# First gate weights next to x, Fox's decay columns as fp32r halves, small transfers on the weight queue, a Silu at the head of each expert slot

## The reference

```python
# first network, layer by layer
x = x + 0.5 * swiglu(rmsnorm(x, norm_g[l, 0]), ffn_w_in[l, 0], ffn_w_out[l, 0])   # width 2816
x = x + (hgrn2_mixer if l == 0 else fox_mixer)(rmsnorm(x, norm_g[l, 1]), ...)
x = x + 0.5 * swiglu(rmsnorm(x, norm_g[l, 2]), ffn_w_in[l, 1], ffn_w_out[l, 1])
# fox_mixer: q, k, v, g, z_f = split(h @ w_in)      # z_f: 16 columns, one per head
#   c = cumsum(log_sigmoid(z_f + b_f)); softmax(q.k * scale + c_t - c_s) @ v, times sigmoid(g)
# second network, layer by layer: nsa_mixer, then mla_mixer
x = layer_norm(ALPHA * x + concat(mixer(x), memory_attention(x)) @ w_out, ...)
x = layer_norm(ALPHA * x + hier_moe(x), ...)        # 4 groups of 4 experts, width 512
```

## Time and profile before

| | us |
|---|---|
| median of three runs | 2218.84 (2216.57 to 2220.15) |
| profiled execution, its own time | 2213.9 |
| its span, first to last instruction | 2212.0 |
| TensorE busy | 2097.1 (95%) |
| VectorE busy | 1481.5 (67%) |
| ScalarE busy | 1158.2 (52%) |
| mean granted TensorE clock | 0.984 of full speed |

### The profile page before, as it was taken

How to read it: one execution, slowest core, us unless ns; L and a number is a source line. 1 busy time by engine, 2 the same in 40 slices (tenths; PEclk the granted TensorE clock), 3 DMA queues, 4 the chain that set the end, 5 groups by cost and what they waited for, 6 DMA issues and landing times. The chain is left out here.

```text
span 2212.0 us, 36828 instructions
## 1 busy us (share of the span) xinstructions
PE 2097.1 (95%) x14195; PEld 1880.7 (85%) x14195; DVE 1481.5 (67%) x2246; ACT 1158.2 (52%) x1657; POOL 26.1 (1%) x34
## 2 busy tenths in 40 slices
PE   6999999999999999889999989999999989999997
PEld 6999898999999978779998977787778758778876
DVE  5655675665666644476564447789888466888896
ACT  4343533534444335474433336677776455777774
POOL 1000000000000020000000000000000000000000
PEclk9999999999999999999999979999999999999999
DMA  8555222654444533335455421599996515799991
GB/s 280 189 194 186 96 77 96 218 181 171 171 171 171 184 102 122 129 132 171 171 179 153 146 77 65 189 327 331 344 316 213 218 39 172 247 328 325 317 358 57
DMA packets 312310, 421.09 MB, mean 190 GB/s; under 512 B 7844, under 2 KB 266304, under 8 KB 312096
## 3 DMA queue, kind: packets, MB, share of 16 engines
q1 hardware_dynamic: 308864, 415.93, 55.2%
q10 hardware_dynamic: 2816, 2.38, 0.5%
q0 software_dynamic: 544, 1.62, 0.3%
HBM read 416.70 MB, written 1.05 MB: 189 GB/s over the span
## 5 line engine op out<-in xcount | busy, mean ns | idle before, releaser
L2869 DVE TENSOR_TENSOR w_lo<-weight_ring,w_hi 128x1024 fp32r<-128x1024 f32 x384 | 449.3, 1220 | 36.1 <-ACT w_hi L2718 31.2
L572 PE MATMUL banks<-x_hi,w_hi 128*128 128x256 f32 x1408 | 400.6, 285 | 9.2 <-DVE w_lo L525 8.0
L573 PE MATMUL banks<-x_lo,w_hi 128*128 128x256 f32 x1408 | 399.0, 283 | 0.0
L574 PE MATMUL banks<-x_hi,w_lo 128*128 128x256 f32 x1408 | 398.9, 283 | 0.0
L2718 ACT ACTIVATE w_hi<-weight_ring 128x1024 fp32r<-128x1024 f32 x384 | 382.2, 1053 | 21.4 <-PE banks L2605 21.4
L518 ACT ACTIVATE w_hi<-weight_ring 128x1024 fp32r<-128x1024 f32 x88 | 93.0, 1057 | 418.2 <-PE banks L574 418.0
L890 DVE TENSOR_TENSOR pieces<-weight_ring,pieces 128x512 fp32r<-128x512 f32 (+2 forms) x245 | 166.8, 689 | 177.4 <-ACT pieces L879 175.8
L572 PEld LDWEIGHTS banks<-x_hi,w_hi 128*128 128x128 f32 x1408 | 270.8, 192 | 11.6 <-DVE w_lo L525 8.9
L879 ACT ACTIVATE pieces<-weight_ring 128x512 fp32r<-128x512 f32 (+2 forms) x245 | 151.4, 627 | 228.6 <-PE banks L826 218.3
L573 PEld LDWEIGHTS banks<-x_lo,w_hi 128*128 128x128 f32 x1408 | 270.9, 192 | 0.1
L574 PEld LDWEIGHTS banks<-x_hi,w_lo 128*128 128x128 f32 x1408 | 270.8, 192 | 0.0
(11 more groups left out here) (367 smaller groups left out, 3890.6 us busy)
## 6 DMA issues: line engine op xcount, KB each, us to landing
weight_ring<-in_ffn_w_in SPq DMA_DIRECT2D x88, 1024.0 KB, 7.5
weight_ring<-in_moe_w_gate SPq DMA_DIRECT2D x64, 1024.0 KB, 6.5
weight_ring<-in_moe_w_up SPq DMA_DIRECT2D x64, 1024.0 KB, 9.0
weight_ring<-in_moe_w_down SPq DMA_DIRECT2D x64, 1024.0 KB, 11.0
weight_ring<-in_ffn_w_out SPq DMA_DIRECT2D x44, 1024.0 KB, 9.6
weight_ring<-in_hg_w_in SPq DMA_DIRECT2D x12, 1024.0 KB, 8.1
weight_ring<-in_fox_w_in SPq DMA_DIRECT2D x12, 1024.0 KB, 8.5
weight_ring<-in_nsa_w_in SPq DMA_DIRECT2D x10, 1024.0 KB, 8.0
```

What stands on the lines that cost most here:

```text
L572: pe.matmul(out, w_hi, m_hi, start=start, stop=False, skip_group_check=True)
L573: pe.matmul(out, w_hi, m_lo, start=False, stop=False, skip_group_check=True)
L574: return pe.matmul(out, w_lo, m_hi, start=False, stop=stop, skip_group_check=True)
L2869: dve.tensor_tensor(self.piece(s, p, self.w_lo), self.piece(s, p), self.piece(s, p, self.w_hi.bitcast(F32)), ALU.subtract).then_inc(sem[ki ...
```

## The change

- **Opening.** TensorE turns x0 before it waits for the rows, and the rows go to another buffer (`cat`). SyncE issues the three transfers of the first fill right behind x and waits for the rows after them; the gate half has a semaphore of its own. ScalarE starts with a Sqrt of zero, waits for the parameters after its first square, splits the gate half of the first tile between chunks 1 and 2 of the input, and the up half and the down weights after the last chunk. VectorE follows in the same order. TensorE's gate half waits for `gate_lo` alone.
- **Hgrn2.** The wait for the whole split input becomes a wait by chunk in the first tile.
- **Fox.** The decay columns are split once, ahead of the norm, and z is made with `pe_three`, two tiles per chunk of the input. Abs and Exp move from q2 to q1; Ln stays at q2. The root for q stands ahead of the Sigmoid of g0, no longer behind it. The eight bias transfers go from ScalarE at g3 to SyncE between the v fills and the output weights.
- **Nsa.** The eight pair transfers go to SyncE between the fill of w1 and that of q0; the eight key transfers go to SyncE ahead of the output weights.
- **Moe.** `act_slot` begins with a Silu of one column into an otherwise unused tile.

The diff, without blank lines, most unchanged lines, and declarations of semaphores:

```diff
@@ -246,6 +246,7 @@
...
+    self.table = f32("table", [P, 1])
@@ -289,7 +290,10 @@
...
+    self.wz_split = f32("fox_w_z_split", [P, 2, KD, FOX_H], F32R)
...
+    self.first_gate, self.gate_hi, self.gate_lo = s("first_gate"), s("gate_hi"), s("gate_lo")
+    self.root_of_zero = f32("root_of_zero", [P, 1])
@@ -336,9 +340,9 @@
...
-    self.rows = k.sq[:].rearrange("p k t -> p (k t)")[:, 0:P]
-    self.pe_rows = k.sq[:].rearrange("p k t -> p (k t)")[0:32, P:2 * P]
-    k.banks.plan("params", "x0", "x1", "x2", "x3")
+    self.rows = k.cat.rearrange("p k t -> p (k t)")[:, 0:P]
+    self.pe_rows = k.cat.rearrange("p k t -> p (k t)")[0:32, P:2 * P]
+    k.banks.plan("x0", "params", "x1", "x2", "x3")
@@ -347,8 +351,6 @@
...
-    eng.wait_ge(k.rows_ready, 12 * 16)
 def act_dma(self, eng):
@@ -384,13 +386,12 @@
     for q in range(4):
-        out = b.claim(pe, f"x{q}") if q else None
-        if q == 0:
+        if q == 1:
             pe.wait_ge(k.rows_ready, 12 * 16)
...
             b.filled(pe.transpose(out[:, P:P + 32], self.pe_rows, k.ident[0:32, 0:32]), "params")
-            out = b.claim(pe, "x0")
+        out = b.claim(pe, f"x{q}")
         for n in range(4):
@@ -398,16 +399,19 @@
 def dve(self, dve):
     k, b = self.k, self.k.banks
-    src = b.wait(dve, "params")
-    dve.tensor_copy(k.param[:, 0:N_ROWS], src[:, 0:N_ROWS])
-    b.read(dve.tensor_copy(k.pe_cols[:], src[:, P:P + 32]), "params")
     for q in range(4):
...
         ins.then_inc(k.x_ready, 1)
+        if q == 0:
+            dve.wait_ge(k.x_ready, 1)
+            b.release(dve, "x0")
+            src = b.wait(dve, "params")
+            dve.tensor_copy(k.param[:, 0:N_ROWS], src[:, 0:N_ROWS]).then_inc(k.params_ready, 1)
+            b.read(dve.tensor_copy(k.pe_cols[:], src[:, P:P + 32]), "params")
     dve.wait_ge(k.x_ready, 4)
-    for q in range(4):
+    for q in range(1, 4):
         b.release(dve, f"x{q}")
@@ -499,12 +503,66 @@
-    with eng.Fori(0, turns) as i:
+    if not self.j0:
+        self.first_load(eng)
+        for f in range(1, half):
+            load(f, 0, 0)
+    with eng.Fori(0 if self.j0 else 1, turns) as i:
         for f in range(half):
...
+def first_load(self, eng):
+    k, r, n = self.k, self.k.ring, self.fills[0]
+    r.wait_free(eng, n)
+    slot, full = r.slot(n), r.full[n % SLOTS]
+    wg, wu, wd = self.sources(0, 0)
+    eng.dma_start(slot[:, 0:2048].rearrange("p (k n) -> p k n", k=KD), wg).then_inc(k.first_gate, 16)
+    eng.dma_start(slot[:, 2048:4096].rearrange("p (k n) -> p k n", k=KD), wu).then_inc(full, 16)
+    eng.dma_start(slot[:, 4096:6144].rearrange("p (j n) -> p j n", j=2), wd).then_inc(full, 16)
+    eng.wait_ge(k.rows_ready, 12 * 16)
+def first_tile(self, w, part):
+    half = slice(part * KD * P, (part + 1) * KD * P)
+    if w is None:
+        raw = self.k.ring.slot(self.fills[0])[:, part * 2048:(part + 1) * 2048]
+        return raw.rearrange("p (k n) -> p k n", n=256)[:, :, 0:P]
+    return w[:, 0, half].rearrange("p (k n) -> p k n", n=P)
+def act_first_gate(self, act):
+    k = self.k
+    act.wait_ge(k.first_gate, 16)
+    act.sem_inc(k.ring.full[self.fills[0] % SLOTS], 16)
+    act.wait_ge(k.gu_ready, 1)
+    act.activation(self.first_tile(k.w_hi, 0), self.first_tile(None, 0), ACT.Copy).then_inc(k.gate_hi, 1)
+def act_first_rest(self, act):
+    k = self.k
+    k.ring.wait_full(act, self.fills[0])
+    act.activation(self.first_tile(k.w_hi, 1), self.first_tile(None, 1), ACT.Copy).then_inc(k.gu_hi, 1)
+    act.wait_ge(k.out_used, 1)
+    raw = k.ring.slot(self.fills[0])[:, 4096:4096 + D]
+    act.activation(k.w_hi[:, 0, 2048:3072], raw, ACT.Copy).then_inc(k.out_hi, 1)
+def dve_first_gate(self, dve):
+    k = self.k
+    dve.wait_ge(k.gate_hi, 1)
+    dve.tensor_tensor(self.first_tile(k.w_lo, 0), self.first_tile(None, 0), self.first_tile(k.w_hi.bitcast(F32), 0),
+                      ALU.subtract).then_inc(k.gate_lo, 1)
+def dve_first_rest(self, dve):
+    k = self.k
+    dve.wait_ge(k.gu_hi, 1)
+    dve.tensor_tensor(self.first_tile(k.w_lo, 1), self.first_tile(None, 1), self.first_tile(k.w_hi.bitcast(F32), 1),
+                      ALU.subtract).then_inc(k.gu_lo, 1)
+    self.dve_split_out(dve, 0, 0)
@@ -575,9 +633,12 @@
 def pe_gate_up(self, pe, b, base, first=False):
     k = self.k
-    pe.wait_ge(k.gu_lo, base + 1)
+    if self.j0 or not first:
+        pe.wait_ge(k.gu_lo, base + 1)
     pe.wait_ge(k.h_ready, base + 1)
     for part in range(2):
+        if first and not self.j0:
+            pe.wait_ge(k.gu_lo if part else k.gate_lo, 1)
         for kk in range(KD):
@@ -626,14 +687,20 @@
         tiles = slice(2 * c, 2 * c + 2)
+        if not self.j0 and c == 2:
+            self.act_first_gate(act)
         act.wait_ge(k.x_ready, 4 * (self.turn - 1) + c + 1)
         act.activation(k.sq[:, tiles], k.x[:, tiles], ACT.Square).then_inc(k.norm_sq, 1)
+        if not self.j0 and c == 0:
+            act.wait_ge(k.params_ready, 1)
         for kk in (2 * c, 2 * c + 1):
...
 def dve_input(self, dve):
...
     for c in range(4):
+        if not self.j0 and c == 2:
+            self.dve_first_gate(dve)
         for kk in (2 * c, 2 * c + 1):
@@ -648,9 +715,12 @@
 def act(self, act):
...
         self.act_split(act, 0, self.j0, 0)
+    else:
+        act.wait_ge(self.k.zero_ready, 1)
+        act.activation(self.k.root_of_zero[:], self.k.zeros[:, 0:1], ACT.Sqrt)
     self.act_input(act)
     if not self.j0:
-        self.act_split(act, 0, self.j0, 0)
+        self.act_first_rest(act)
     self.act_std(act)
@@ -676,8 +746,7 @@
     if not self.j0:
-        self.dve_split_gu(dve, 0, self.j0)
-        self.dve_split_out(dve, 0, self.j0)
+        self.dve_first_rest(dve)
     dve.wait_ge(k.norm_std, self.ffn + 1)
@@ -1101,10 +1170,9 @@
 def pe(self, pe):
...
     self.norm.pe(pe)
-    self.pe_wait_input(pe)
     for part in "zq":
         for n in range(4):
-            self.pe_columns(pe, f"hg_{part}{n}")
+            self.pe_columns(pe, f"hg_{part}{n}", self.in_split if part == "z" and n == 0 else None)
     i = 0
@@ -1541,18 +1609,25 @@
                       ).then_inc(k.ring.full[n % SLOTS], 16)
+    eng.wait_ge(self.c_ready, 5)
+    eng.wait_ge(self.bias_ready, 4)
+    for half in range(2):
+        for row, to, src in ((0, self.bq, self.c_hi), (1, self.bq, self.c_lo), (32, self.bk, self.n_hi), (33, self.bk, self.n_lo)):
+            row += half * HD
+            eng.dma_start(to[row:row + 1].bitcast(F32), src[half:FOX_H:2, :].bitcast(F32)).then_inc(self.bias_rows, 16)
     self.sp_out(eng)
 def pe(self, pe):
...
     self.norm.pe(pe)
-    self.pe_wait_input(pe)
-    pe.wait_ge(k.small_ready, k.small_all)
+    pe.wait_ge(self.wz_ready, 2)
     out = b.claim(pe, "fox_z")[0:FOX_H, 0:T]
     for kk in range(KD):
-        for part in range(2):
-            last = pe.matmul(out, k.wz[:, kk], k.half[1 - part][:, kk].bitcast(F32), start=kk == 0 and part == 0,
-                             stop=kk == KD - 1 and part == 1)
+        if kk % 2 == 0:
+            pe.wait_ge(k.xs_lo, 4 * self.in_split + kk // 2 + 1)
+        last = self.pe_three(pe, out, (k.wz_split[:, 0, kk], k.wz_split[:, 1, kk]), (k.half[1][:, kk], k.half[0][:, kk]),
+                             kk == 0, kk == KD - 1)
     b.filled(last, "fox_z")
@@ -1583,6 +1658,8 @@
 def act(self, act):
     k, b = self.k, self.k.banks
+    act.wait_ge(k.small_ready, k.small_all)
+    act.activation(k.wz_split[:, 0], k.wz[:], ACT.Copy).then_inc(self.wz_ready, 1)
     self.norm.act_squares(act)
@@ -1602,6 +1679,8 @@
         src = b.wait(act, name).rearrange("p (h t) -> p h t", h=2)
+        if name == "fox_g0":
+            root("q")
         if part == "g":
@@ -1609,29 +1688,24 @@
             b.read(act.activation((self.kk if part == "k" else self.q)[:, hs], src, ACT.Copy), name)
-        if name in ("fox_q0", "fox_g0"):
-            root("k" if part == "q" else "q")
-        if name == "fox_q2":
+        if name == "fox_q0":
+            root("k")
+        if name == "fox_q1":
...
             act.activation(self.ez, self.ez, ACT.Exp, scale=-1.0).then_inc(self.z_step, 1)
+        if name == "fox_q2":
             act.wait_ge(self.z_step, 3)
             act.activation(self.ez, self.ez, ACT.Ln, bias=k.const(C_ONES, 1, FOX_H)).then_inc(self.z_step, 1)
-        if name == "fox_g3":
-            act.wait_ge(self.c_ready, 5)
-            act.wait_ge(self.bias_ready, 4)
-            for half in range(2):
-                for row, to, src in ((0, self.bq, self.c_hi), (1, self.bq, self.c_lo), (32, self.bk, self.n_hi), (33, self.bk, self.n_lo)):
-                    row += half * HD
-                    act.dma_start(to[row:row + 1].bitcast(F32), src[half:FOX_H:2, :].bitcast(F32)).then_inc(self.bias_rows, 16)
     self.act_units(act)
...
 def dve(self, dve):
     k, b, seq = self.k, self.k.banks, self.k.dve_seq
+    dve.wait_ge(self.wz_ready, 1)
+    dve.tensor_tensor(k.wz_split[:, 1], k.wz[:], k.wz_split[:, 0].bitcast(F32), ALU.subtract).then_inc(self.wz_ready, 1)
```

(28 more changed lines are left out.)

## The result

The changed kernel took 2189.26 us (median of four, 2188.64 to 2189.89), the kernel before beside it 2219.49 (2216.57 to 2223.69); the ratio is 0.9866, with a 95% interval of 0.9846 to 0.9887. That is 30.2 us less; two repetitions (runs 1 and 10) gave 24.9 and 25.7. The two profiled executions lie 25.3 apart, 2213.9 and 2188.64: the one before was the lowest of its five, while the four after lie within 1.3 us of each other. 2189.26 lies inside the range, and just above its lower end of 2189.

A forecast was written before the change was run, and what follows sets the result against it. TensorE, busy 95% of the span and working in one fixed order, was taken as the bound. Removed waits of 6.9 + 6.0 + 1.3 + 0.9 + 2.85 + 3.9 = 21.8 us gave 2197.0 us, range 2189 to 2206.

The forecast's parts named there:

- Opening 6.9: Opening: third gate-up starts at 35.6 instead of 42.51, a gain of 6.9 us, the later of two limits.
- the data side's working: Opening: filling the DMA hole brings the second fill 3.9 us forward to 31.4, so the third gate-up starts at 35.6.
- rows late: Opening rival: parameter rows land behind the whole first fill (14.4), opening gains only 3.5, total 2200.4 us; chance 0.12.
- no data limit: Opening rival: compute side rules, opening gains 9.7, in all 24.6, total 2194.2 us; chance 0.08.
- Fox's z 6.0: Fox's decay columns: 24 fp32r matmuls starting chunk by chunk gain 6.0 us; bounds 3.1 and 6.4.
- Table loads and root order, 1.3 and 0.9: Fox: moving Abs and Exp to q1 gains 1.3 us, the root ahead of g0's Sigmoid 0.9.
- Transfers, 2.85 and 3.9: Small transfers moved from ScalarE to SyncE remove TensorE waits: 2.85 us in Fox, 3.9 in Nsa.
- Removed waits come back: Rival: TensorE, fed earlier, waits again close behind; gain only 15.3 us in all, total 2203.5; chance 0.12.
- Slots and Hgrn2, 0: Expert slots' moved table load and Hgrn2's finer wait: each gives 0.
- The rival of a longer table switch: Expert slots: a switch holds ScalarE as long again as its load, 7.4 us more gain, total 2189.6; chance 0.03.
- Slower: Rival: SyncE, waiting for keys or biases, holds back weights queued behind it, total 2229 us; chance 0.03.
- taken off the median: Final step: the summed gain subtracted from the three-run median 2218.84, 4.9 above the profiled execution, giving 2197.0 us.

The follow-up runs named there:

- run 1: The changed kernel again, no edit, beside the kernel before: median 2191.6 us, ratio 0.9881.
- run 10: The changed kernel a third time, no edit, beside the kernel before: median 2191.4 us, ratio 0.9872.
- run 6: Changed kernel with GpSimd's constants and small loads issued only after the second down product: 2187.8 us, one execution.
- run 3: Changed kernel with Fox's z by plain fp32 matmuls and the wait for the whole split input, as before: median 2195.6 us.
- run 5: Changed kernel with Fox's old ScalarE order (Abs and Exp at q2, root for q behind the Sigmoid of g0): 2192.7 us, one execution.
- run 4: Changed kernel with the 24 small transfers of Fox and Nsa back on ScalarE: median 2205.1 us.
- run 11: Kernel before with only the 24 small transfers of Fox and Nsa moved to SyncE: median 2207.9 us, ratio 0.9948 to the kernel before.
- run 9: Changed kernel without the Silu heading each expert slot, and with Hgrn2's first matmul waiting for the whole split input: median 2189.7 us.
- run 2: Changed kernel with the whole opening as before: median 2197.2 us.
- run 7: Changed kernel with SyncE waiting for the parameter rows right behind the gate transfer, before up and down weights: 2202.0 us, one execution.
- run 12: Kernel before with only the new opening: median 2211.9 us, ratio 0.9972 to the kernel before.

## Why the prediction was right, and where it was short

**The sum.** Forecast 21.8. At equal clock the changed kernel is 20.7 to 22.4 faster (22.4 for the first four executions, set against the kernel before of the later groups); the trace of before and that of run 1, which lost the same to the clock in all (32.4 up to the last products), are 21.6 apart there. What the forecast says at equal clock is less than 21.8, for the opening's stretch at half clock is part of its 6.9 and the fit takes it out: 21.8 less 0.78 x 3.4 is 19.1. So the kernel gained some 1.6 to 3.3 more than was forecast. Term by term:

- *Opening 6.9:* measured 6.7 to 7.2 at the third gate-up over four traces. The size is right, and so is the data side's working: 31.04 for 31.4, 35.33 for 35.6. The allowance was about right as well: I wrote that up to 2.8 us of delay of the rows is free, and they were 2.6 late in the first trace and 3.1 in run 1 (11.35), where the third gate-up came 0.3 later. I had called the prediction wrong if rows land after 11; in most traces they did (up to 11.37 in run 10), and it cost no more than 0.5. The rival *rows late* (14.4) did not come, and *no data limit* was tested by run 6: without it the delay of the rows is the limit, not 9.7. What failed is the first gate matmul, said for 16.6 and measured at 18.50. The Trainium skill (DMA: Bandwidth & Descriptors, "Latency and other measured facts") gives HBM access as 2 us at high load, from which came my estimate near 10 for the rows. With 1 MB behind x they landed at 9.91 and 10.24, which agrees; with 3 MB at 10.84 to 11.37, which is later.
- *Fox's z 6.0:* 5.9 to 6.0 by run 3 and between the first traces. The matmuls with 16 weight columns start 0.116 apart, as the full ones do, not twice that.
- *Table loads and root order, 1.3 and 0.9:* waits of 1.31 and 0.71, worth 1.6 and 0.7 by run 5, 2.3 in all.
- *Transfers, 2.85 and 3.9:* the waits were 2.85 and 3.87 and left whole, worth 7.5 in place of 6.75. *Removed waits come back* is refuted by runs 4 and 11.
- *Slots and Hgrn2, 0:* 0 by run 9. The rival of a longer table switch would have shown there: without the Silu each slot has one switch more, and is no longer. Of all the figures said in advance its 2189.6 lies nearest to the measured 2189.26, and that is coincidence. By the Trainium skill (ScalarE: Activation LUTs, "What ACT_TABLE_LOAD costs") a drain of about 1.4 comes with a switch; in the rows above the next instruction starts 0.02 behind the end of the load, and the trace shows no drain.
- *Slower:* SyncE was held nowhere; the earlier trace rows and the queue above have the same issues as before, some 13 us earlier in Fox.

**What was short.** Between the mean spans of the executions in the table (the first four of the changed kernel among them), 2216.0 and 2188.5, lie 27.5, not 21.8. The measured terms add up to 7.0 + 6.0 + 2.3 + 7.5 = 22.8. Then the kernel before loses 8.0 us more to the clock; 3.4 of it is the stretch in the opening, inside the 7.0 already; the other 4.6 at 0.78 is 3.6. Together 26.4; 1.1 is unplaced. (The traces of runs 2 and 11, also with the old opening, lose 5.1 in it and are 7.9 and 7.5 late; with their figures the sum is 25.6 to 26.0.) The step that failed is "taken off the median": I took the profiled execution's sum off the median as if the 4.9 between them were common to both kernels, and put the clock at nothing. Instead the kernel before loses more to the clock in most of its executions, 38.4 on average against 35.4 in the profiled one, and the changed kernel does not: 30.5 against 28.4 in its first profiled one.

**Where luck comes in.** The range reached down to 2189 because it took in a compute-limited opening (24.6) and the 4.9 between execution and median. The opening did not gain that rival's 9.7; what filled the room was above all the clock. And 30.2 was the largest of the three differences between medians.

**What stays open.** Why it loses less. No run ties the part outside the opening to a single edit: the transfers alone leave 37.1, the opening alone 34.9 (as much less as its own stretch), and the changed kernel with one part put back loses 32.5, 30.7 and 33.7. Such a mean is good to 1.0 to 1.6, but only to 3 for the last two, whose executions lost from 24 to 42. So a sum of small shares would look like this, and so would one share of the transfers that needs the rest. The stretches lie mostly at the same places in both traces, the mixers and above all the sparse attention. Which of them are longer in the executions of before with 40 us lost can't be said, since none of those was profiled. Two other traces lost about as much: in run 11 (39.8) a stretch of 10.2 us at half clock stands at 1863, in run 7 (39.6) one of 10.2 at 1378; the trace of before has none there.

## What to carry to other kernels

When two chains meet, work out both and how much slack one has against the other: here 2.6 us of delay cost nothing beside a data limit, lifting the data limit alone gave nothing, and both together gave one microsecond. Small transfers that an engine issues between its computations are best counted as waits of whoever needs that engine next; moved to a queue with nothing urgent behind it, they were worth all of it and some tenths more for each wait. Before reading a few microseconds off medians, set each execution's granted clock beside its time; at equal clock a scatter of 1.3 us was left where the executions of one kernel ranged over 12.

## What was not expected of the hardware

- Executions of one kernel on one chip differ by some 10 us with the clock: before, 2212.5 to 2224.8, with 31 to 44 us lost (runs 9 to 12); 0.78 of each microsecond lost shows in the time.
- 1 MB of weights behind x holds up the twelve small row transfers more than half as long as 3 MB do: landed at 8.2 to 8.5 with none, 9.9 to 10.2 with 1 MB, 10.8 to 11.4 with 3 MB.
- GpSimd's constants and strided small loads (1.6 MB) delayed the second fill by 6.7 to 7.1 us: from 21 to 28 all queues together moved 303 to 329 GB/s with them and 367 without.
